# High and low weight parts side by side in one tensor, in a two-block transformer kernel on one core

## The reference

```python
x = x + parallel_mixer(rmsnorm(x, norm_mix_g), ...) ; x = x + memory_cross_attention(...)
h = rmsnorm(x, norm_ffn_g)
x = x + jnp.square(jax.nn.relu(h @ w_ff1)) @ w_ff2          # 1024 -> 4096 -> 1024
h = jnp.concatenate([meta, x], axis=1)                      # 272 positions
h = h + 0.5 * swiglu(rmsnorm_2(h, n1), w_gate, w_up, w_down)  # 1024 -> 2816 -> 1024
u = rmsnorm_2(h, mix_norm) ; h = h + mixed(u @ w_in) @ w_out
h = h + 0.5 * swiglu(rmsnorm_2(h, n2), w_gate, w_up, w_down)
return rmsnorm_2(h, final_norm)[:, 16:]
```

## Time and profile before

| what | value |
|---|---|
| median of 3 runs | 922.28 us (922.0 to 922.43) |
| profiled execution: span from first to last instruction | 918.1 us |
| mean granted TensorE clock | 0.998 |
| PE busy, PEld busy | 98%, 97% |
| DVE busy, ACT busy | 70%, 58% |
| DMA | 157.37 MB, mean 171 GB/s |

### The profile page before, as it was taken

The page is one execution under the profiler, slowest core; times in us unless marked ns, Lnnn a source line. Parts: engine busy times, 40 slices in busy tenths (PEclk is TensorE's granted clock), DMA queues, the critical chain, the costliest instruction groups (busy, mean ns, idle before and its releaser), DMA issues.

```text
span 918.1 us, 18474 instructions
## 1 busy us (share of the span) xinstructions
PE 903.7 (98%) x7443; PEld 886.4 (97%) x7443; DVE 641.5 (70%) x1092; ACT 528.2 (58%) x862; POOL 3.5 (0%) x9
## 2 busy tenths in 40 slices
PE   8999999999999999999999999999999999999996
PEld 7988999899999999999999999999999999999996
DVE  6999787776546666667665648768669877767553
ACT  6798876776446655544443435444675665454452
POOL 1000000000000000000000000000000000000000
PEclk9999999999999999999999999999999999999999
DMA  9652426265665566555556565554416656666641
GB/s 330 227 165 70 138 93 206 61 216 185 231 191 171 197 199 192 174 175 176 171 178 204 162 178 162 156 176 128 149 51 194 194 184 185 196 200 198 210 138 47
DMA packets 110292, 157.37 MB, mean 171 GB/s; under 512 B 9728, under 2 KB 61056, under 8 KB 110080
## 3 DMA queue, kind: packets, MB, share of 16 engines
q1 hardware_dynamic: 109632, 155.22, 53.6%
q10 hardware_dynamic: 576, 0.96, 0.3%
HBM read 155.11 MB, written 1.05 MB: 170 GB/s over the span
## 4 chain that ended last, share of the span: by engine, by line
PE 95%; DVE 2%; ACT 1%; DMA 1%; issue 0%; SPq 0%; DVEq 0%; ACTq 0%
PE ps L1055 29%; PE ps L1057 29%; PE ps L1056 29%; PE ps L1102 1%; PE ps L1138 1%; DMA raw<-d_small 1%; PE ps L1314 0%; PE ps L1334 0%; PE ps L1272 0%; PE ps L1335 0%; DVE wl L1820 0%; PE ps L1294 0%; PE ps L1148 0%; DVE S L2067 0%; PE ps L1085 0%
## 5 line engine op out<-in xcount | busy, mean ns | idle before, releaser
L1820 DVE TENSOR_TENSOR wl<-raw,wh 128x1024 fp32r<-128x1024 f32 (+2 forms) x291 | 346.0, 1212 | 193.1 <-ACT wh L1393 192.8
L1393 ACT ACTIVATE wh<-raw 128x1024 fp32r<-128x1024 f32 (+2 forms) x291 | 298.5, 1046 | 194.5 <-PE ps L1057 192.6
L1055 PE MATMUL ps<-U,wh 128*128 128x256 f32 (+2 forms) x1392 | 398.5, 286 | 2.2 <-DVE wl L1820 2.2
L1057 PE MATMUL ps<-U,wl 128*128 128x256 f32 (+2 forms) x1392 | 391.2, 281 | 0.0
L1056 PE MATMUL ps<-UL,wh 128*128 128x256 f32 (+2 forms) x1392 | 390.4, 280 | 0.0
L1055 PEld LDWEIGHTS ps<-U,wh 128*128 128x128 f32 (+1 forms) x1392 | 261.9, 188 | 5.6 <-DVE wl L1820 2.9
L1056 PEld LDWEIGHTS ps<-UL,wh 128*128 128x128 f32 (+1 forms) x1392 | 262.0, 188 | 2.1 <-issue 1.4
L1057 PEld LDWEIGHTS ps<-U,wl 128*128 128x128 f32 (+1 forms) x1392 | 261.6, 188 | 0.0
L1055 PE MATMUL ps<-H,wh 128*128 128x256 f32 (+1 forms) x736 | 207.7, 282 | 0.0
L1057 PE MATMUL ps<-H,wl 128*128 128x256 f32 (+1 forms) x736 | 205.7, 280 | 0.0
L1056 PE MATMUL ps<-HLO,wh 128*128 128x256 f32 (+1 forms) x736 | 205.5, 279 | 0.0
(11 more groups left out here) (337 smaller groups left out, 789.6 us busy)
## 6 DMA issues: line engine op xcount, KB each, us to landing
raw<-w_ff SPq DMA_DIRECT2D x64, 512.0 KB, 4.2
raw<-ffn_w_gate SPq DMA_DIRECT2D x88, 256.0 KB, 3.6
raw<-ffn_w_up SPq DMA_DIRECT2D x88, 256.0 KB, 4.3
raw<-ffn_w_down SPq DMA_DIRECT2D x44, 512.0 KB, 4.5
raw<-w_in SPq DMA_DIRECT2D x40, 512.0 KB, 4.4
raw<-w_out SPq DMA_DIRECT2D x16, 512.0 KB, 4.8
raw<-wkv_x SPq DMA_DIRECT2D x8, 512.0 KB, 3.7
raw<-w_in SPq DMA_DIRECT2D x9, 256.0 KB, 3.2
```

Source lines behind the costliest of these rows:

```text
L1055: e.matmul(out, sh, xh, start=(i == 0 and n == 0), stop=False)
L1057: mm = e.matmul(out, sl, xh, start=False, stop=(over and n == nk - 1))
L1393: e.activation(wh, raw, ACT.Copy).then_inc(*up("w_hi", v))
L1820: lo = e.tensor_tensor(wl, raw, wh.bitcast(F32), ALU.subtract)
```

## The change

`wh` and `wl` become one tensor `wp` of the same total size, with four places of 2 x 1152 columns. Column c of the high part lies at element 2c of the place, column c of the low part at 2c + 1, so that each part is read and written with a step of 8 bytes. ScalarE writes the even elements of a place; VectorE reads them and writes the odd ones of the same place; `low_half` goes. The weight load reads 128 columns over 1024 bytes where it read them over 512. `first_columns` places row blocks with the new widths in steps of 64 bytes as before, so a high part still starts 64 bytes further than the activation tile that streams during its load, modulo 256, and a low part 68 bytes. The two matmuls of each half of `latent_values`, where a weight is the moving operand (six matmuls of 512 columns in all), read it with the same step.

In the built programs each engine has the same instructions in the same order with the same waits before and after; the access patterns of the weight parts differ and nothing else.

```diff
-        while skew is not None and (n * width // 16 + shift - k - skew) % 4:
+        while skew is not None and (n * width // 8 + shift - k - skew) % 4:
             shift += 1
-        at.append(n * width + 16 * shift)
+        at.append(n * width + 8 * shift)
...
-def low_half(half):
-
-    return half ^ 1
-
-
-def split_blocks(parts, half, name, g, i):
+def split_blocks(pairs, which, half, name, g, i):
+
...
-    return parts[:, half, at[0]:at[0] + len(at) * step].rearrange("p (k c) -> p k c", c=step)[:, :, 0:width]
+    blocks = pairs[:, half, 2 * at[0]:2 * (at[0] + len(at) * step)].rearrange("p (k c n) -> p k c n", c=step, n=2)
+    return blocks[:, :, 0:width, which]
...
-        wh, wl = split_blocks(t["wh"], h, name, g, i), split_blocks(t["wl"], low_half(h), name, g, i)
+        wh, wl = (split_blocks(t["wp"], which, h, name, g, i) for which in range(2))
...
-        wh, wl = (rows4(t[n][:, a, 0:1024])[:, :, 128:256] for n, a in (("wh", half), ("wl", low_half(half))))
+        wh, wl = (t["wp"][:, half, 0:2048].rearrange("p (h c n) -> p h c n", h=4, n=2)[:, :, 128:256, which]
+                  for which in range(2))
...
-    return raw, split_blocks(t["wh"], half, name, g, i), split_blocks(t["wl"], low_half(half), name, g, i)
+    return raw, split_blocks(t["wp"], 0, half, name, g, i), split_blocks(t["wp"], 1, half, name, g, i)
...
-        t["wh"] = sb("wh", [P, NHL, PITCH], F32R)
-        t["wl"] = sb("wl", [P, NHL, PITCH], F32R)
+        t["wp"] = sb("wp", [P, NHL, 2 * PITCH], F32R)
```

## The result

The kernel after takes 956.24 us (median of 4 runs, 954.76 to 956.37) against 922.14 us (4 runs, 921.9 to 922.43) of the kernel before beside it: ratio 1.0368, interval 1.0355 to 1.0381. It is slower by 34 us. A gain of 24 us was forecast.

The account below looks back on a forecast made before the run. TensorE's matmul pace was taken as the bound, slowed by its two SBUF reads meeting. Gains of 11.8, 4.6 and 7.3 us, some 24, take the profiled span from 918.1 to 894, 898 us with 4.2 around it; range 879 to 958.

Parts of the forecast that it names:

- the first of the change part by part: Weight loads on TensorE: at the moving tile's speed they need not meet it; 24 us gained in sum, chance 0.50.
- the 111 ns: Distance between weight loads with nothing to stream, taken as the new pace of 256-column matmuls, from 113.3 ns.
- three gains: TensorE: 11.8 us on 256-column matmuls, 4.6 us on the slow ones among them, 7.3 us on 272 columns.
- the formerly slow thousand: About 1,000 matmuls of 256 columns running near 118 ns, expected to gain another 4.6 ns each, 4.6 us.
- The bound under it: TensorE's matmul pace: time above streaming was taken for interference between SBUF reads of next weight part and moving tile.
- The best end: TensorE: only 2 ns per matmul above streaming remain, 108.7 ns for 256 columns; 43 us gained, time 879 us.
- the 6.6 ns: Part of each 256-column matmul's 113.3 ns on TensorE that is not streaming, which needs 106.7 ns.
- a rival at 0.12: TensorE: 6.6 ns may belong to the hand-over between weight sets, not the reads; no change, 922 us, chance 0.12.
- The bad end: TensorE: every load collides as in products uq and ukv, 120.0 ns per matmul; 41 us more.
- 427 or fewer matmuls: Count in a 50 us stretch of 256-column work (117.7 ns or more) that would show the two reads colliding.
- that rival: Lock-step collision on TensorE: reads at equal speed stay in one part of SBUF; 941 to 963 us, chance 0.26.
- Loads at half speed: TensorE: a load needing two reads per column takes 210 ns, pace 213 ns; 680 us more, about 1,600, chance 0.04.
- The third rival: Splits too dear: strided access costs VectorE 1.07 us more on each of 78 splits; 942 us, chance 0.08.

Follow-up runs that it names:

- loads8: Kernel before with only the weight loads reading at a step of 8 bytes, layout and splits untouched, output wrong: 955.5 us, ratio 1.036.
- pair_s3: Kernel after with all weight blocks 192 bytes later, so high parts start 0 bytes from the streaming tile, modulo 256: 952.5 us, ratio 1.034.
- pair_32: Kernel after with all weight blocks 32 bytes later, so high parts start 96 bytes further than the streaming tile: 959.7 us, ratio 1.042.
- pair_s1: Kernel after with all weight blocks 64 bytes later, so high parts start 128 bytes further than the streaming tile: 957.1 us, ratio 1.040.
- pair_s2: Kernel after with all weight blocks 128 bytes later, so high parts start 192 bytes further than the streaming tile: 955.6 us, ratio 1.037.
- loads12: Kernel before with weight loads at a step of 12 bytes (8 where the block is narrower than 384 columns), output wrong: 1303.5 us.
- loads16: Kernel before with weight loads at a step of 16 bytes where the block holds 512 columns, 8 elsewhere, output wrong: 1703.5 us, ratio 1.849.
- loads0: Kernel before with weight loads reading one element 128 times in the four down-projections, output wrong: 921.9 us, ratio 1.001.
- splits8_even: Kernel after with loads of 128 neighbouring elements, all from element 0 (64 bytes further), splits still strided, output wrong: 922.7 us, ratio 1.001.
- plain_s3: Kernel before with all weight blocks 192 bytes later, so loads start 0 bytes from the streaming tile, modulo 256: 951.4 us, ratio 1.032.
- both16: Kernel before with every load starting 16 bytes later, 80 bytes further than the streaming tile, output wrong: 947.9 us, ratio 1.028.
- plain_s1: Kernel before with all weight blocks 64 bytes later, so loads start 128 bytes further than the streaming tile: 947.9 us, ratio 1.030.
- plain_s2: Kernel before with all weight blocks 128 bytes later, so loads start 192 bytes further than the streaming tile: 943.4 us, ratio 1.025.
- low4: Kernel before with only low-part loads starting 4 bytes later, 68 bytes further than the streaming tile, output wrong: 944.9 us, ratio 1.025.
- loads8_low: Kernel before with a step of 8 bytes in low-part loads only, one load in three, output wrong: 952.4 us.

## Why the prediction was wrong

**The step that failed** is the first of the change part by part, "With 8 bytes per column it covers 1024 bytes in 105 ns, 9.7 bytes per ns, the speed of the moving tile. Starting 64 or 68 bytes further, it stays about there and need not be met." From that the pace was to fall to the 111 ns at which loads can follow each other. The runs put this in its place: a load with the step has a record of 194 to 195 ns instead of 188, the pace is 120.0 ns although nothing but the loads' step is changed (loads8), and no start tried helps (0, 64, 96, 128 and 192 bytes further give 120.0 to 120.7 ns in pair_s3, the kernel after, pair_32, pair_s1 and pair_s2). The 9.7 bytes per ns that the step counted on are about the limit of a load: loads12 and loads16 ask for more and pay for all of it. The forecast's three gains, 11.8, 4.6 and 7.3 us, were losses of 28.8 us for 256 columns, which include the formerly slow thousand, and 4.9 us for 272.

**The bound under it** was wrong too. The best end, and the 111 ns too, took the surplus over streaming for something that can go. loads0 shows that the 6.6 ns stay even when a load reads a single element. The evidence was in the prediction: loads of 32 columns had not made their matmuls faster. I gave it to a rival at 0.12 and set it aside for the earlier trace rows, which show that the pace can be worse than 113.3, not that it can be better.

**The bad end was right in size.** "Every load collides as in rows 9" was priced at 120.0 ns and 41 us. The 256-column work has that 120.0 ns to a tenth. The 272-column work lost 2.7 ns per matmul and not 6.7, so the sum is 34 us, not 41. By the prediction's own sign (427 or fewer matmuls) the 419 measured are the collision. The reason given (two reads at equal speed stuck in the same part of SBUF) did not hold, since at 8 bytes five different starts give the same pace within 0.7 ns. That the price held is luck as far as the runs show: 120.0 ns was read at another start and a step of 4 bytes, where other bad starts give 117.6 and 118.8 ns. (1.4 x 5,136 in that rival is 7.2, not 7.3; nothing rests on it.)

**Loads at half speed** came true not at 8 bytes but at 16, with 233 ns for a forecast of 213.

**The splits.** "The durations ... should cost nothing" was right for VectorE (1214 ns) and wrong for ScalarE (1148 instead of 1046 ns), and that did no harm: splits8_even has 1132 ns and 922.7 us. The third rival falls.

**`latent_values`** was bounded at 1.3 us for twice the time, and that is what it cost.

**The Trainium skill's rule** that two accesses per 16-byte line run at full speed (SBUF — State Buffer, Door 1, the note on cachelines) left the sum as it was. For loads the traces agree in part: at a step of 8 bytes their records are 6 to 7 ns longer (194 to 195 for 188), and at 12 and 16 bytes they pay in proportion to the lines, as that note has it for accesses that enter a new line. For a moving operand in fp32r the trace does not agree: two columns per group take nearly twice the time (440 to 470 ns for 230 to 240).

What stays open: why a step of 8 bytes, whose 64 groups fit into the load's time, still costs 6.7 ns per matmul; why one load in three is enough; why the start at 64 bytes is the good one at 4 bytes; and why 272 columns never come below 123 ns on average. The change is traced to the step of the loads, not to a mechanism.

## What to carry to other kernels

When TensorE is busy throughout, read its pace from the number of matmuls in a stretch, before anything else: here a loss of 3.7% showed in no wait and no busy share. Count how far each of its two operands is spread, and keep 32-bit weight loads and above all 32-bit moving operands at neighbouring columns. Before undoing a surplus, take its supposed cause away once in an experiment, even one that leaves the right product out; one such run (a load of one element) would have shown that the reads' spread was not what held the pace.

## What the runs showed of the hardware

- The pace of matmuls of 256 columns in fp32r depends on where the next weight load starts relative to the streaming tile, modulo 256 bytes: 113.3 ns at 64, 117.6 to 120.0 at 0, 80, 128 and 192 (plain_s3, both16, plain_s1, plain_s2). Even at 64 about a thousand matmuls run near 118 ns. Four bytes in every third load cost 5.2 ns per matmul on average (low4).
- A weight load with a step of 8 bytes has a record of 194 to 195 ns for 188, whatever its neighbours do (loads8_low), and in one load of three it is enough for a pace of 120.0 ns.
- From a step of 8 bytes to 12 and 16 a weight load costs TensorE 1.67 and 1.88 ns more per matmul for each further 16 bytes that it covers (loads12, loads16); a moving operand at a step of 8 bytes takes 1.7 to 1.8 ns for each 16 bytes (`latent_values`).
- The paces 113.3, 120.0, 173.3 and 233.3 ns are 17, 18, 26 and 35 times 6.67 ns, which is 16 columns at 106.7 ns per 256. The paces between, as 117.6 and 118.5 ns, are no such multiples; the single steps in them vary (115 to 122 ns in low4).
- A write with a step of 8 bytes costs ScalarE 8 to 10% (1132 and 1148 ns for 1046); VectorE reads and writes with it at no cost (1214 for 1212).
